# Hybrid diffusion layer on one core: the first adaLN columns computed by quarters, with three FFN weight units worked on in between

## What is computed

```python
ml = jnp.split((jax.nn.silu(c) @ ada_w[i] + ada_b[i])[:, None, :], N_MOD, axis=-1)
mc = jnp.split((jax.nn.silu(c_ctx) @ ada_w[i] + ada_b[i])[None, None, :], N_MOD, axis=-1)
x = ffn_sublayer(x, ml[0], ml[1], ml[2], ffn1_norm[i], ffn1_w_gate[i], ffn1_w_up[i], ffn1_w_down[i])
ctx = ffn_sublayer(ctx, mc[0], mc[1], mc[2], ffn1_norm[i], ...)
...
def ffn_sublayer(t, shift, scale, gate, norm_g, w_gate, w_up, w_down):
    h = modulate(rms_norm(t, norm_g), shift, scale)      # h * (1 + scale) + shift
    return t + gate * (MACARON_WEIGHT * swiglu(h, w_gate, w_up, w_down))
```

## Time and profile before

| | |
|---|---|
| median of 3 runs | 1355.36 us (1354.34 to 1355.42) |
| span of the profiled execution | 1354.2 us |
| median less that span | 1.2 us |
| busy share of the span | PE 98%, DVE 64%, POOL 48%, ACT 30% |
| first x_in matmul | 9.61 us |
| first FFN matmul | 40.94 us |
| joint stage of units 0 and 1 ends | 58.5 us |

### The profile page before, as it was taken

The page is one execution under the profiler, slowest core; times in us unless marked ns, Lnnn a source line. Parts: engine busy times, 40 slices in busy tenths (PEclk is TensorE's granted clock), DMA queues, the critical chain, the costliest instruction groups (busy, mean ns, idle before and its releaser), DMA issues.

```text
span 1354.2 us, 21460 instructions
## 1 busy us (share of the span) xinstructions
PE 1333.5 (98%) x8546; PEld 1229.7 (91%) x8546; DVE 865.3 (64%) x1376; ACT 400.0 (30%) x757; POOL 651.0 (48%) x408
## 2 busy tenths in 40 slices
PE   5999999999999999999999999999999999999998
PEld 4899999999999999998888888888998999999997
DVE  5787368568556555437656649826778765555666
ACT  4320010210210110124635321222142555544455
POOL 1544444543543533532732356636467455655554
PEclk9999999999999999999999999999999999999999
DMA  9553354353444344223322479484736233344322
GB/s 357 161 148 85 121 148 120 120 157 116 126 135 139 102 126 158 62 55 109 80 62 52 126 212 259 152 266 148 229 87 199 63 94 94 107 115 114 101 72 85
DMA packets 236782, 178.18 MB, mean 132 GB/s; under 512 B 33416, under 2 KB 211852, under 8 KB 236684
## 3 DMA queue, kind: packets, MB, share of 16 engines
q1 hardware_dynamic: 216624, 145.78, 37.6%
q10 hardware_dynamic: 20060, 31.04, 7.0%
HBM read 156.93 MB, written 19.86 MB: 131 GB/s over the span
## 4 chain that ended last, share of the span: by engine, by line
PE 93%; DVE 3%; DMA 2%; SPq 1%; issue 1%; ACT 0%; DVEq 0%; ACTq 0%
PE ps L1244 47%; PE ps L1971 13%; PE ps L1566 13%; PE ps L2030 7%; DMA ada_w<-in_ada_w_dram 2%; PE ps L1255 1%; PE ps L1844 1%; DVE ada_acc L2860 1%; DVE ps L2972 1%; PE ps L2057 1%; PE ps L1881 1%; PE ps L1669 1%; PE ps L1487 1%; PE ps L1438 1%; PE ps L1706 1%
## 5 line engine op out<-in xcount | busy, mean ns | idle before, releaser
L1143 POOL TENSOR_SCALAR w_hi<-w_raw 128x1024 fp32r<-128x1024 f32 x128 | 153.4, 1198 | 527.8 <-PE ps L1244 276.0
L1146 POOL TENSOR_TENSOR w_lo<-w_raw,w_hi 128x1024 fp32r<-128x1024 f32 x128 | 325.4, 2542 | 10.7
L1244 PE MATMUL ps<-h_hi,w_lo 128*128 128x384 f32 (+2 forms) x1000 | 291.4, 351 | 0.0
L1244 PE MATMUL ps<-h_hi,w_hi 128*128 128x384 f32 (+2 forms) x1000 | 287.1, 346 | 0.0
L1244 PE MATMUL ps<-h_lo,w_hi 128*128 128x384 f32 (+2 forms) x1000 | 287.0, 346 | 0.0
L1244 PEld LDWEIGHTS ps<-h_hi,w_lo 128*128 128x128 f32 x1000 | 178.8, 188 | 14.9 <-issue 4.3
L1244 PEld LDWEIGHTS ps<-h_lo,w_hi 128*128 128x128 f32 x1000 | 180.6, 188 | 10.5
L1244 PEld LDWEIGHTS ps<-h_hi,w_hi 128*128 128x128 f32 x1000 | 180.4, 188 | 10.7
L1222 POOL TENSOR_TENSOR w_lo<-w_raw,w_hi 128x512 fp32r<-128x512 f32 x90 | 115.6, 1297 | 105.7 <-ACT w_hi L2609 104.2
L2860 DVE SCALAR_TENSOR_TENSOR ada_acc<-ada_w,cs,ada_acc 128x1024 f32<-128x1024 f32 x70 | 108.3, 1581 | 7.8 <-DMA ada_w<-in_ada_w_dram 5.5
L1971 PE MATMUL ps<-h_hi,w_hi 128*128 128x256 f32 x360 | 102.0, 283 | 0.0
(11 more groups left out here) (459 smaller groups left out, 2635.0 us busy)
## 6 DMA issues: line engine op xcount, KB each, us to landing
w_raw<-in_ffn_w_gate_dram SPq DMA_DIRECT2D x44, 512.0 KB, 5.1
w_raw<-in_ffn_w_up_dram SPq DMA_DIRECT2D x44, 512.0 KB, 4.1
w_raw<-in_ffn_w_down_dram SPq DMA_DIRECT2D x44, 512.0 KB, 4.5
ada_w<-in_ada_w_dram ACTq DMA_DIRECT2D x32, 512.0 KB, 3.9
w_raw<-in_w_in_dram SPq DMA_DIRECT2D x32, 512.0 KB, 4.3
ada_w<-in_ada_w_dram SPq DMA_DIRECT2D x30, 512.0 KB, 4.3
c_scr<-cp ACTq DMA_DIRECT2D x16, 288.0 KB, 3.8
b_scr<-bt_sb ACTq DMA_DIRECT2D x16, 256.0 KB, 3.9
```

The source lines that it names most:

```text
L1143: pool.tensor_scalar(w_hi[:, s, 0:cols], w_raw[:, s, 0:cols], 1.0, 1.0, ALU.mult, ALU.mult)\
L1146: pool.tensor_tensor(w_lo[:, s, 0:cols], w_raw[:, s, 0:cols], w_hi[:, s, 0:cols].bitcast(F32), ALU.subtract).then_inc(w_split, 1)
L1244: last = pe.matmul(mv[2], st, mv[part], start=(first and q == 0), stop=(n == len(terms) - 1 and q == 2))
```

## The change

The columns of groups 0 and 1 are made in four quarters of 256 columns (the k pair 2q, 2q+1 of both), and h with them. A quarter is two DMAs of 1 MB in pieces of 1024 bytes. SP queues x, quarter 0, units 0, 1 and 2, quarters 1 and 2, and quarter 3 after the row products of quarter 1. Three units are joint instead of two; their steps are written out by hand with the row products and the turning of quarters 1 to 3, and turn_lambda, in between. Row products put four k on the four strips; a matmul with strip_eye adds the strips while it turns a row. x is turned tile by tile as it lands, 8 transposes each. DVE scales and shifts in one instruction per k and token kind, and ACT's h_hi is a plain copy, one instruction per k. The six small loads (S5 parameters, gla_norm) go behind h_hi 0 and 1 in ACT's queue, and ACT loads its table for the root early. POOL no longer waits for row1 and for h_lo. The unit slots' later contents, the order of DVE's queue behind h_lo, and everything after the first units are unchanged.

```diff
-PLAIN = KD // 2
+PLAIN = 5
+QUARTERS = 4
+QW = D // QUARTERS
...
-JOINT_FROM = 2
+JOINT = 3
...
-_number(JOB, [("vec", 1), ("x", KD), ("spread", 1), ("row1", 1), ("col1", 1), ("row0", 1), ("col0", 1), ("lam", 1), ("skip", 1),
+_number(JOB, [("x_first", 4), ("vec", 1), ("x_rest", 2), ("skip", 3), ("spread", 1), ("open", 1),
...
+    quarter_at = ((h_at + 32 * KB, h_at + 40 * KB), (scratch_at + 32 * KB, scratch_at + 24 * KB), (ada_at, scratch_at + 40 * KB))
+    ada_q = [[place(f"ada_q{b}_{g}", [P, KD, QW], F32, at=quarter_at[b][g]) for g in range(2)] for b in range(3)]
...
-            for k in range(KD):
-                sp.dma_start(first_tile(1, k), ada_src(1, k)).then_inc(ada_here0[1][k], 16)
             first_src = [a[w][0].rearrange("(k p) c -> p k c", p=P) for w in ("ffn1_w_gate", "ffn1_w_up")]
-            sp.dma_start(raw(0, KD, P), first_src[0][:, :, 0:P]).then_inc(w_here[0], 16)
-            for k in range(KD):
-                sp.dma_start(first_tile(0, k), ada_src(0, k)).then_inc(ada_here0[0][k], 16)
-            sp.dma_start(raw(1, KD, P), first_src[1][:, :, 0:P]).then_inc(w_here[1], 16)
+
+            def first_unit(v):
+                sp.dma_start(raw(v, KD, P), first_src[v % 2][:, :, P * (v // 2):P * (v // 2) + P]).then_inc(w_here[v], 16)
+
+            ada_cols_src = a["ada_w"][0].rearrange("(k p) c -> p k c", p=P)
+
+            def quarter(q):
+                for g in (1, 0):
+                    c = g * D + q * QW
+                    sp.dma_start(quarter_tile(g, q)[:, :, :], ada_cols_src[:, :, c:c + QW]).then_inc(ada_here0[g][q], 16)
+
+            quarter(0)
+            first_unit(0)
+            first_unit(1)
+            first_unit(2)
+            quarter(1)
+            quarter(2)
+            sp.wait_ge(row_made, 2)
+            quarter(3)
...
-                        if with_ada and part.segs + i == 0 and v < 2:
+                        if with_ada and part.segs + i == 0 and v < JOINT:
                             continue
                         s = (u0 + v) % 4
                         sp.wait_ge(w_split, n + (v + 1))
                         sp.dma_start(raw(s, KD, P), gu_src[v % 2][:, :, bass.ds(i * (SEG * P) + (f0 + v // 2) * P, P)])\
                             .then_inc(w_here[s], 16)
                         if with_ada and part.segs + i == 0:
+                            if v == 3:
+                                sp.wait_ge(row_made, 3)
...
-                        if fresh and n < 4:
-                            is_done(pool, JOB["row1"])
-                            if n == 2:
-                                pool.wait_ge(h_ok, KD)
-                        else:
+                        if not fresh or n >= 4:
...
+            def row_products(q, g):
+
+                j = JOB["open"]
+                if g and q:
+                    pe.wait_ge(row_ok, q)
+                pe.wait_ge(ada_here0[g][q], 16)
+                for k in range(KD):
+                    r = STRIP * (k % 4)
+                    last = pe.matmul(lat(j)[r:r + STRIP, QW * g:QW * g + QW], cs_wide[:, k, :], quarter_tile(g, q)[:, k, :],
+                                     start=(k < 4), stop=(k >= 4))
+                if g == 0:
+                    last.then_inc(row_made, 1)
+
+            def turn_rows(q):
...
+                        last = pe.matmul(ctx_(j)[:, at:at + 2], ada_row[:, q % 2, QW * g + P * c:QW * g + P * c + P], strip_eye[:, 0:2],
...
+                last.then_inc(cols_made, 1)
...
+            pe.wait_ge(consts, 11)
+            for t in range(4):
+                turn_x(t)
+            turn_vecs()
+            for t in range(4, 6):
+                turn_x(t)
+            spread_roots()
+            wait_read(pe, JOB["open"])
+            wait_read(pe, JOB["ffn1"])
             pe.wait_ge(silu_c, 1)
-            row_products(1, 0, 4)
-            spread_roots()
-            row_products(1, 4)
-            pe.wait_ge(row_ok, 1)
-            turn_row(1, 1)
-            row_products(0, 0, KD - 1)
-            turn_lambda()
-            row_products(0, KD - 1)
...
-                    for v in range(joint):
+                    def joint_start(v):
                         pe.wait_ge(w_split, un + (v + 5))
                         slot_free(js.gu(v))
...
+
+                    def joint_step(vs, k):
+                        for v in vs:
+                            joint_hi(v, k)
+                        for v in vs:
                             joint_lo(v, k)
...
+
+                    if joint:
+                        joint_start(0)
+                        joint_start(1)
+                        joint_step((0, 1), 0)
+                        joint_step((0, 1), 1)
+                        row_products(1, 1)
+                        row_products(1, 0)
+                        joint_start(2)
+                        joint_step((2,), 0)
+                        turn_rows(1)
+                        joint_step((2,), 1)
+                        joint_step((0, 1, 2), 2)
+                        row_products(2, 1)
+                        row_products(2, 0)
+                        joint_step((0, 1), 3)
+                        turn_rows(2)
+                        joint_step((2,), 3)
+                        joint_step((0, 1, 2), 4)
+                        row_products(3, 1)
+                        row_products(3, 0)
+                        joint_step((0,), 5)
+                        turn_rows(3)
+                        joint_step((1, 2), 5)
+                        joint_step((0, 1, 2), 6)
+                        turn_lambda()
+                        joint_step((0, 1, 2), 7)
...
+            act.wait_ge(consts, 11)
+            act.activation(oms[:, 0:1], eps[:, :], ACT.Sqrt)
+            for t in range(6):
                 row_squares(t)
             act.wait_ge(ms_ok, 6)
             act.activation(root[:, :], root[:, :], ACT.Sqrt, bias=eps[:, :], scale=1.0 / D).then_inc(root_ok, 1)
...
-                    for k in range(PLAIN):
-                        for c, v in ((slice(0, NL), 0), (slice(NL, NT), 1)):
-                            ins = act.activation(scaled[:, k, c], scaled[:, k, c], ACT.Copy, scale=amul[:, 0, k, v:v + 1])
-                        ins.then_inc(xn_ok, 1)
+            j = JOB["vec"]
+            is_done(act, j)
+            act.activation(vt[:, :], lat(j)[:, 0:P], ACT.Copy).then_inc(slot_read[j % 4], 2)
+            was_read(act, j)
+            for v, row in enumerate((104, 112)):
+                ins = act.activation(cs_wide[:, :, v], vt[:, row:row + 8], ACT.Silu)
+            ins.then_inc(silu_c, 1)
+            for v, row in enumerate((104, 112)):
+                ins = act.activation(cs[:, :, v], vt[:, row:row + 8], ACT.Silu)
+            ins.then_inc(silu_c, 1)
+
+            def small_loads():
...
+
+            for q in range(QUARTERS):
+                act.wait_ge(row_made, q + 1)
+                if q >= 2:
+                    act.wait_ge(cols_made, q - 1)
+                act.activation(ada_row[:, q % 2, :], lat(JOB["open"]), ACT.Copy).then_inc(row_ok, 1)
+                for k in (2 * q, 2 * q + 1):
+                    act.wait_ge(xn_ok, k + 1)
+                    act.activation(h_hi[:, k, :], scaled[:, k, :], ACT.Copy).then_inc(h_hi_ok, 1)
+                if q == 0:
+                    small_loads()
...
+            def quarter_mod(q):
+
+                c = slice(2 * q, 2 * q + 2)
+                dve.wait_ge(cols_made, q + 1)
+                by_group = mod[:, 0:2 * KD, :].rearrange("p (g k) v -> p g k v", g=2)[:, :, c, :]
+                bias = vt[:, 0:2 * KD].rearrange("p (g k) -> p g k", g=2)[:, :, c].unsqueeze(3).to_broadcast([P, 2, 2, 2])
+                link(TT(by_group, open_cols(q), bias, ALU.add))
+                last = STT(amul[:, 0, c, :], mod[:, KD + 2 * q:KD + 2 * q + 2, :], 1.0,
+                           vt[:, 72 + 2 * q:74 + 2 * q].unsqueeze(2).to_broadcast([P, 2, 2]), ALU.add, ALU.mult)
+                if q < QUARTERS - 1:
+                    link(last)
+                else:
+                    last.then_inc(cols_ok, 1)
+                    dve.wait_ge(cols_ok, 1)
+                for k in (2 * q, 2 * q + 1):
+                    for t, v in ((slice(0, NL), 0), (slice(NL, NT), 1)):
+                        last = TS(scaled[:, k, t], scaled[:, k, t], amul[:, 0, k, v:v + 1], mod[:, k, v:v + 1], ALU.mult, ALU.add)
+                    last.then_inc(xn_ok, 1)
+
+            def quarter_low(q):
+
+                for k in (2 * q, 2 * q + 1):
+                    dve.wait_ge(h_hi_ok, k + 1)
+                    TT(h_lo[:, k, :], scaled[:, k, :], h_hi[:, k, :].bitcast(F32), ALU.subtract).then_inc(h_ok, 1)
+
+            for t in range(6):
+                j = x_job(t)
                 is_done(dve, j)
-                dve.tensor_copy(x[:, k, :].rearrange("p (b c) -> p b c", b=2), both(j, 384)).then_inc(slot_read[j % 4], 1)
```

(28 more changed lines are left out.)

194 lines of the change are left out of this document (64 added, 130 removed).

## The result

The changed kernel takes 1372.68 us (median of 4, 1369.95 to 1374.76) against 1355.29: the ratio is 1.0129, with a 95% interval of 1.0114 to 1.0143. It is slower, as predicted, but by 17.4 us and not by 8; the prediction's range ended at 1369. The span of the profiled execution is 1373.0 us, 18.8 more than before; it is the slowest of the four (1374.8 us), so what is read from its rows adds up to a little more than the medians differ by.

What follows compares the result with a forecast made beforehand. PE was taken as the bound, 98% busy, its first FFN matmul late behind 8.4 MB of ada_w. The profiled span 1354.2 + 6.3 (later sums) + 1.7 (half clock) = 1362.2 us gave a median of 1363, range 1352 to 1369.

Steps and rivals of the forecast that it cites:

- The bound that hung on whether a scaling with two column operands waits for POOL: Part 1: if DVE's new scaling instructions do not wait for POOL, k = 0 and 1 end at 32.6 us, not 34.6.
- Part 1: Opening up to the first FFN matmuls: those of k = 0 and 1 end near 34.6 us, partly at half clock.
- the bound of 36: Part 1: upper bound for the end of the k = 0 and 1 matmuls, if all run at half clock: 36 us.
- Part 2: The joint jobs of three units: turn_lambda done at 63.5 us, joint stage at 66.7, against 66.9 before.
- rival C: Slower than forecast: unit 3's split falls on quarter 2, act_lo 0 too late for unit 5; 1366 to 1368 us, 15%.
- Part 3: DVE's queue behind h_lo, through the last adds: done 45.4 us after turn_lambda; PE needs them at 38.8.
- The sum: First ada sum 6.3 us later after a 6.6 us PE wait, half clock costing 1.7: 1362.2 us span.
- the opening itself wins almost nothing (0.2): Part 2: joint stage ends 0.2 us sooner; the 13 us earlier start carries 8.4 us of added matmuls and waits.
- signs named in advance: Profile after: first matmul 27 to 28 us, joint stage 64 to 67, s5 copies near 63, ada_acc wait 4 to 8.

Runs made afterwards that it cites:

- e3: The changed kernel with 22 instead of 6 filler products ahead of the first joint matmul; 1374.8 us.
- e9: The kernel before, with five memsets in DVE's queue directly ahead of the last two additions of group 2; 1368.3 us.
- e10: e9 with 15 products that feed nothing ahead of PE's wait for the sums; 1360.2 us.
- e13: e9 with the sixteen ada sums in one group behind fifteen of the matmul pairs, instead of interleaved; 1362.4 us.
- e6: The changed kernel with lambda and angle ahead of quarter 3, 22 instead of 6 fillers, unit 3's split held until quarter 3 of h is made; 1357.9 us.
- e14: e6 with quarter 0 scaled by ACT, 18 fillers, and row products of quarters 1 to 3 one or two joint products sooner; 1351.0 us.
- e1: The changed kernel with group 2's running sums adding only 64 of 1024 columns from the third slice on; 1359.9 us.
- e2: The changed kernel with 15 products that feed nothing ahead of PE's wait for the last sum of group 2; 1370.6 us.

## Why the prediction was right or wrong

Right: slower, and by the mechanism named, DVE's queue too late for the sums. The wait for DVE ada_acc is there, 3.33 us at 113.7; h_hi 0 was put at 27.5 and the first FFN matmul came at 27.62; DVE's chain behind `turn_lambda` was put at 45.4 us and took 42.3 (113.58 - 71.3), act_lo of the first pair at +19.1 for +19.6. The bound that hung on whether a scaling with two column operands waits for POOL is settled: 7.13 us against 1.65. By what the Trainium skill says of the ports that DVE and GpSimd share (SBUF — State Buffer, Who interferes with whom: a tensor_scalar between SBUF tensors can take them, and the other engine is then blocked for the whole instruction) it was to be expected, and the trace agrees.

The rate of the 512-byte pieces was right: 288 to 302 GB/s from 18 to 22 us, where units 0 to 2 were landing. Unit 0 was put at 19.1 and POOL began to split it at 19.49. The Trainium skill (DMA: Bandwidth & Descriptors, Specifications) names 512 bytes as enough for full rate. At the 420 GB/s of the 4096-byte pieces, an estimate, a unit would take 1.2 us instead of 1.8, so units 0 to 2 would land 0.5 to 1.6 us earlier, and not 0.9 to 2 as the prediction has it; the trace doesn't show such a rate for them.

Wrong: the size. The span came out 10.8 us over the sum (1373.0 for 1362.2), the median 9.7. In the terms of the sum:

- Part 1, k = 0 and 1 done at 34.6: 36.5. All of it ran at half clock, which was the bound of 36 and half a microsecond more.
- Part 2, quarter by quarter from there, 5.9 us more than its sum: 0.7 in quarter 1, 4.7 in quarter 2, 0.5 in quarter 3. Of the 4.7, 1.7 is the split of unit 3 on quarter 2 (a wait of 2.75 for 1.1), which the prediction priced at up to 2.4 and gave to rival C. 2.8 is the half clock behind that wait (the matmuls of k = 4 took 5.9 us for 3.15), which it did not price at all. The other 1.4 us are spread over many instructions. `turn_lambda` was done at 71.3 instead of 63.5, 7.8 later.
- Part 3: DVE's chain was 3.1 us shorter than its sum. 1.5 of it lies in the last two adds, which took 3.26 us and not 4.8, because POOL's split began just behind their start (see e3), and 1.0 in the split of unit 7, which came when the adds of tile 4 were almost done.
- The sum: the wait of 6.6 us was 3.3, and this is DVE's shorter chain. PE's lateness has no part in it, since both count from `turn_lambda`: PE needed 39.1 us for 38.8. The half clock behind it was priced at 3.4 us of matmuls, 1.7 lost, by the one row there was, a wait of 2.46 us followed by row products of 256 columns and fillers of 128, none of one column. It lasted 17.1 us and cost 16.2 - 9.5 = 6.7 up to the first down product and 1.3 behind it. This is the term that failed: 8.0 instead of 1.7. e9 and e10 measure it at 8.0 in the kernel before, and e13 shows what the row left out: what stands behind the wait.

7.8 - 3.1 + 6.3 = 11.0 us, and the span was missed by 10.8. So two terms were mis-sized, the opening by 7.8 and the half clock at the sums by 6.3, and the shorter chain hid 3.1 of it by luck.

The sentence "the opening itself wins almost nothing (0.2)" was too kind. The joint stage ended 7.6 us later than in the kernel before, and 1.3 later in e6, with the clock up. e14, where it ended at 61.75, 5.1 sooner, shows that this was a matter of its order and of DVE's place in it, not of the quarters. Of the signs named in advance, the first matmul, the long scaling instructions and the half clock were there. The end of the joint stage (64 to 67, it was 74.5), DVE's copies (near 63, 71.4), and the length of the wait (4 to 8, 3.3) were not.

Of the rivals, C came nearest: its first half happened, its second (act_lo too late for unit 5) did not.

Two things stay open. The same opening runs differently from one execution to the next, and why was not tried. In the changed kernel's profile the clock was 0.50 for 10.2 and 6.8 us and the joint stage ended at 74.5. In those of e1 and e2 it was 0.50 for 3.4, 6.7 and 3.4 us (from about 15.6, 29.5 and 43.1 in e1), the split of unit 3 missed quarter 2, and the joint stage ended at 71.7 and 71.9. And e13 shows that the interleaved sums hold the clock down, not which property of them does.
